# Small matmuls of the recurrent inverse and state chain: one per pair of heads, or one per head in its own column group

## The chip, the cores and the metric

The kernel runs on one core of a Trainium2 chip. The metric is the device time of one launch in microseconds (us), median of three runs; lower is better.

## What is computed

One decoder layer over 528 tokens (16 meta tokens and 512 tokens of the input) of width 2048. A normalised input goes through one large projection. Half of its columns feed sixteen RWKV-7 heads of width 64, the other half eight differential-attention heads; both results are gated, joined, projected again, normalised and added to the input. Cut to what matters here, the recurrent half is, for each head,

```python
def step(S, inp):
    r_t, w_t, k_t, v_t, kk_t, b_t = inp
    sa = jnp.einsum('bhvk,bhk->bhv', S, -kk_t)
    S = S * w_t[:, :, None, :] + sa[..., None] * b_t[:, :, None, :] + v_t[..., None] * k_t[:, :, None, :]
    y = jnp.einsum('bhvk,bhk->bhv', S, r_t)
    return S, y
_, ys = lax.scan(step, S0, (tm(r), tm(decay), tm(k), tm(v), tm(kk), tm(b)))
```

The kernel does this scan by chunks of 64 tokens: in each chunk a triangular 64x64 matrix has to be inverted for each head, and the states go from chunk to chunk.

## The kernel before

The matmul engine (PE) multiplies in two kinds of instruction: a load of the stationary operand into its 128x128 array, and a matmul that streams the moving operand past it. In the profile each plain fp32 matmul of the code stands as two load records and two matmul records; one of type fp32r (a rounded fp32) or fp16 stands as one of each.

**Projections.** `feature_tile` (L547) is most of PE's work: for 65 tiles of 128 output features it takes 16 slices of the contraction, each with three products (high times high, high times low, low times high), all 128 rows by 128 columns, streaming 528 tokens as two matmuls of 264 or 512 tokens as one. The output projection (L807 to L809, L870 to L872) does the same with 512 columns at a time.

**The recurrent part** is done for pairs of heads, eight pairs in all (`NP_`), one pair in each iteration of an outer list `ITER`, while the features of the next pair are projected. The two heads of a pair lie in the top 64 and the bottom 64 partitions (`halves`). Of the 9 chunks (`NC`) each `GC` = 3 make a group, so there are 24 groups in the kernel.

- `inv_pe` inverts the matrices of one group. For each chunk the two heads' 64x64 matrices stand as the diagonal blocks of one 128x128 block matrix, whose other blocks are zero. All its tensors (`x16`, `xt16`, `z16`, `ab_hi`, `ab_lo`, `lv`, fp16) are 3 x 128 = 384 columns wide. After six fp32 matmuls with 64 rows and 128 columns (L646) comes a first transposition (L653), then five levels, each with three matmuls into `zz` (L667), three into `x` (L679) and three into `xt` (L686), a residual with nine (L692 to L694) and a last product with six (L700, L701). Between them VectorE (DVE, `inv_dve`: L1499, L1511, L1514) and ScalarE (ACT, `inv_act`: L1036, L1059, L1062) take the results out of the accumulator `ma`.
- `chain_pe` carries the state. For each chunk it has five fp32 matmuls 128x128x128: g (L723), a first part of the output (L725, not in the first chunk), u (L728), the new state (L733, not in the last chunk) and a second part of the output (L736, not in the first). `chain_dve` and `chain_act` (L1523, L1528, L1538, L1081, L1088) take the results out of `mb`.

**What sets the order.** Every engine's program is a fixed list, written out by generators. Each step of `inv_pe` and `chain_pe` yields a place, and `upto` emits it between two products of a projection, when the projection has come to that place (`feature_tile` calls it after each product, `place - 1 + part / 3`). So PE leaves the projection for one step, does its 1 to 9 small matmuls and goes back. Semaphores (`wait_ge`) hold a step until its operands are there. For one group `inv_pe` has 13 such steps with matmuls that the change touches: the transposition, five times `zz`, five times `x` and `xt` together, the residual, the last product. `chain_pe` has three for each chunk: g with the first output part, u, and the state with the second output part.

Of the kernel before, what the change touches and what calls it, by code (L numbers as in the profile page):

```python
# [34 lines left out]
P = 128  # L35
# [7 lines left out]
HD = 64  # L43
# [40 lines left out]
def constants():  # L84
# [12 lines left out]
    levels = [ident]  # L97
    m = 1
    while m < CH:
        levels.append(same & ((s // (2 * m)) == (t // (2 * m))) & ((s // m) % 2 == 0) & ((t // m) % 2 == 1))  # L100
        m *= 2
    levels[1] = levels[1].astype(np.float32) - ident
    inside = np.broadcast_to((np.arange(TP) % CH != 0)[None, :], (P, TP))
    f16 = np.concatenate(levels + [inside, -ident], 1).astype(np.float16)
# [19 lines left out]
def hybrid_layer(nc, x, meta_tokens, pre_norm_w, w_in, rwkv_mu, rwkv_w0, rwkv_w_up, rwkv_a0, rwkv_a_up,  # L124
# [3 lines left out]
    with ctx:  # L128
# [14 lines left out]
        c16 = sb("c16", [P, (2 + LEVELS) * P + TP], F16)  # L143
# [56 lines left out]
        t_t = several(2, "t_t", GC * P)  # L200
        b_in = several(NG, "b_in", GC * 2 * P)
        b_in3 = [v.rearrange("p (c t) -> p c t", c=GC) for v in b_in]
        b_in5 = [v.rearrange("p (c k h t) -> p c k h t", c=GC, k=2, h=2) for v in b_in]
        state0 = carve("rwkv", "state0", HD)
        g_sb = carve("rwkv", "g_sb", P)
# [6 lines left out]
        lv = carve("rwkv", "lv", (LEVELS - 1) * GC * P, F16)  # L212
        ab_hi = carve("rwkv", "ab_hi", GC * P, F16)
        ab_lo = carve("rwkv", "ab_lo", GC * P, F16)
        x16 = carve("rwkv", "x16", GC * P, F16)
        xt16 = carve("rwkv", "xt16", GC * P, F16)
        z16 = carve("rwkv", "z16", GC * P, F16)
# [47 lines left out]
        def c16v(k):  # L265
            return c16[:, k * P:(k + 1) * P]

        ident, ident16 = c32v("ident"), c16v(0)
        inside = c16[:, (1 + LEVELS) * P:(1 + LEVELS) * P + TP]
        minus16 = c16[:, (1 + LEVELS) * P + TP:]  # L270
        level_masks = c16[:, P:(1 + LEVELS) * P].rearrange("p (l t) -> p l t", l=LEVELS)
# [262 lines left out]
        def _(pe):  # L534
# [100 lines left out]
            def inv_pe(i, g):  # L635
                n = groups_so_far(i, g)
                cs = [g * GC + c for c in range(GC)]
                bl = lambda v, c: v[:, c * P:(c + 1) * P]
                bank = lambda k, c: ma[:, k * 512 + c * P:k * 512 + (c + 1) * P]
# [12 lines left out]
                for c in range(GC):  # L652
                    last = mm(bank(0, c), bl(xt16, c), ident16, start=True, stop=True)  # L653
                last.then_inc(s("t0_done"), 1)
                for c in range(GC):
                    if cs[c] < SC:
                        last = nc.tensor.transpose(bank(1, c), bk[:, cs[c], :], ident)
                last.then_inc(s("bk_turned"), 1)
                for l in range(1, LEVELS):
# [6 lines left out]
                    for c in range(GC):  # L666
# [569 lines left out]
        def _(dve):  # L1236
# [75 lines left out]
            for v in b_in:  # L1312
                V.memset(v, 0.0)
# [384 lines left out]
```

## Time and profile before

| what | us |
|---|---|
| median of 3 runs | 1394.71 (1393.51 to 1394.75) |
| the profiled execution | 1395.48 |
| its span in the profile | 1393.7 |
| PE matmul busy | 1329.2 |
| PE weight load busy | 1136.1 |
| VectorE busy | 731.8 |
| ScalarE busy | 673.1 |
| GpSimd busy | 304.8 |

PE's matmuls are pipelined and their ends are modelled, so two neighbouring records overlap; the distance from one start to the next is what a matmul costs. Times in a timeline are from the start of the span. "x3" in a timeline row means that three records of one form follow one another and are merged into a row.

### The profile page before, as it was taken

The page shows a single profiled execution, that of the slowest core. Times are in us where ns is not written, and L with a number is a line of the kernel's source. Part 1 is how long each engine was busy: PE and PEld are TensorE (multiplying, and loading weights), DVE is VectorE, ACT ScalarE, POOL GpSimd, SP SyncE. Part 2 cuts the span into 40 slices and gives each one's busy share as a digit, 9 for nine tenths or more (in the row PEclk, how much of TensorE's full clock was granted, in tenths as well). Part 3 has the DMA queues.
Part 4 walks back from the last instruction along what each step waited for, and adds up shares of the span by engine and source line. Part 5 has one row for each costly group of instructions (what it writes and reads, how often), then busy time and mean ns, then how long its engine had stood idle before and what let it go on. Part 6 is the DMA issues. An engine that isn't in the chain of part 4 may idle for free.

```text
span 1393.7 us, 24026 instructions
## 1 busy us (share of the span) xinstructions
PE 1329.2 (95%) x9393; PEld 1136.1 (82%) x9393; DVE 731.8 (53%) x1653; ACT 673.1 (48%) x1550; POOL 304.8 (22%) x234
## 2 busy tenths in 40 slices
PE   3999999999999999999999999999999999989997
PEld 3988888797888879889788877898888988768885
DVE  5346767767677686866866433433343333530013
ACT  4435656556565555656555544444443444432331
POOL 3330001000000100001000323333334333334544
PEclk9999999999999999999999998999999999999998
DMA  6221121111112111111112222222222222235333
GB/s 211 71 76 56 47 63 40 56 54 47 56 46 63 47 54 51 51 56 47 53 47 61 83 63 61 71 81 71 75 76 76 69 76 76 67 92 203 109 93 141
DMA packets 151264, 102.24 MB, mean 73 GB/s; under 512 B 6398, under 2 KB 140640, under 8 KB 149600
## 3 DMA queue, kind: packets, MB, share of 16 engines
q1 hardware_dynamic: 151152, 100.71, 24.3%
q8 instruction: 75, 1.23, 0.4%
q14 instruction: 37, 0.30, 0.1%
HBM read 96.49 MB, written 4.19 MB: 72 GB/s over the span
## 4 chain that ended last, share of the span: by engine, by line
PE 83%; DVE 9%; ACT 4%; issue 3%; POOL 1%; DMA 0%; DVEq 0%; ACTq 0%; SPq 0%
PE tile L547 48%; PE tile L807 2%; PE tile L808 2%; PE tile L809 2%; PE ma L773 2%; PE ma L646 2%; PE ma L686 1%; PE ma L679 1%; PE mb L788 1%; PE ma L667 1%; DVE arena L1499 1%; PE mb L790 1%; PE ma L809 1%; PE mb L807 1%; PE ma L807 1%
## 5 line engine op out<-in xcount | busy, mean ns | idle before, releaser
L547 PE MATMUL tile<-hn_hi,w_hi 128*128 128x264 f32 (+1 forms) x1696 | 446.6, 326 | 0.3
L547 PE MATMUL tile<-hn_hi,w_lo 128*128 128x264 f32 (+1 forms) x1696 | 438.6, 322 | 2.2 <-ACT arena L1062 2.2
L547 PE MATMUL tile<-hn_lo,w_hi 128*128 128x264 f32 (+1 forms) x1696 | 437.8, 321 | 0.0
L885 ACT CAST w_hi<-w_raw 128x512 fp32r<-128x512 f32 x324 | 200.4, 619 | 365.3 <-PE tile L547 254.9
L1177 POOL TENSOR_TENSOR w_lo<-w_raw,w_hi 128x512 fp32r<-128x512 f32 x196 | 255.1, 1302 | 448.3 <-ACT w_hi L885 448.2
L547 PEld LDWEIGHTS tile<-hn_hi,w_hi 128*128 128x128 f32 x1696 | 276.5, 190 | 29.2 <-issue 10.2
L547 PEld LDWEIGHTS tile<-hn_hi,w_lo 128*128 128x128 f32 x1696 | 276.3, 190 | 18.8 <-ACT arena L1062 3.6
L547 PEld LDWEIGHTS tile<-hn_lo,w_hi 128*128 128x128 f32 x1696 | 276.2, 190 | 11.6 <-issue 2.2
L1192 POOL TENSOR_TENSOR arena<-arena,power 128x10 f32<-128x10 f32 (+3 forms) x28 | 43.9, 1569 | 620.3 <-DVE arena L1356 471.2
L1499 DVE TENSOR_TENSOR arena<-ma,c 128x384 f16<-128x384 f32 x120 | 66.7, 556 | 45.9 <-PE ma L667 44.6
L1436 DVE TENSOR_TENSOR w_lo<-w_raw,w_hi 128x512 fp32r<-128x512 f32 x128 | 87.5, 683 | 1.3
L1059 ACT ACTIVATE arena<-ma 128x384 f16<-128x384 f32 x120 | 58.8, 490 | 46.3 <-PE ma L679 45.0
L1599 DVE TENSOR_SCALAR arena<-mb,arena 128x128 f32<-128x128 f32 x32 | 11.2, 350 | 91.9 <-PE mb L790 91.9
L807 PE MATMUL tile<-w_hi,hn_hi 128*128 128x512 f32 x128 | 53.1, 415 | 5.5 <-DVE hn_lo L1618 5.5
L1062 ACT ACTIVATE arena<-ma 128x384 f16<-128x384 f32 x120 | 58.3, 486 | 0.0
L808 PE MATMUL tile<-w_lo,hn_hi 128*128 128x512 f32 x128 | 51.6, 403 | 0.0
L809 PE MATMUL tile<-w_hi,hn_lo 128*128 128x512 f32 x128 | 51.5, 403 | 0.0
L1483 DVE TENSOR_TENSOR arena<-arena,c 128x384 f16<-128x384 f16 x144 | 49.0, 350 | 0.8
L1587 DVE TENSOR_TENSOR ma<-ma,c 128x128 f32<-128x128 f32 x32 | 9.6, 299 | 75.1 <-PE mb L773 75.1
L679 PE MATMUL ma<-arena 128*128 128x128 f16 x360 | 41.7, 224 | 3.3 <-DVE arena L1499 2.0
L667 PE MATMUL ma<-arena 128*128 128x128 f16 x360 | 41.6, 224 | 3.2 <-ACT arena L1059 3.1
L1075 ACT ACTIVATE arena<-arena 64x64 f32<-64x64 f32 x112 | 38.5, 344 | 12.0 <-DVE arena L1538 11.2
(262 smaller groups left out, 2090.1 us busy)
## 6 DMA issues: line engine op xcount, KB each, us to landing
w_raw<-w_in SPq DMA_DIRECT2D x260, 256.0 KB, 2.8
w_raw<-w_out SPq DMA_DIRECT2D x64, 256.0 KB, 3.0
big<-x SPq DMA_DIRECT2D x4, 1024.0 KB, 8.0
arena<-x SPq DMA_DIRECT2D x4, 1024.0 KB, 8.6
out<-big SPq DMA_DIRECT2D x3, 1024.0 KB, 3.9
arena<-post_norm_w SPq DMA_DIRECT2D x1, 1024.0 KB, 5.0
out<-big SPq DMA_DIRECT2D x2, 512.0 KB, 3.2
arena<-table_rope SPq DMA_DIRECT2D x2, 264.0 KB, 2.9
```

Of the source, the lines that this page charges most:

```text
L547: last = mm(o[:, at:at + n], w[:, slot, cols], t[:, kt, tok:tok + n], start=(kt == 0 and w is w_hi and t is hn_hi), stop=(kt == KT - 1 and ...
L667: last = mm(bank(0, c), bl(lv, (l - 1) * GC + c), bl(x16, c), start=True, stop=True)
L679: last = mm(bank(0, c), bl(xt16, c), bl(z16, c), start=True, stop=True)
L807: mm(banks[t], hn_hi[:, k, y], w_hi[:, k % RING, :], start=(k == 0), stop=False)
L808: mm(banks[t], hn_hi[:, k, y], w_lo[:, k % RING, :], start=False, stop=False)
L809: last = mm(banks[t], hn_lo[:, k, y], w_hi[:, k % RING, :], start=False, stop=(k == KT - 1))
L885: nc.scalar.copy(w_hi[:, slot, :], w_raw[:, slot, :]).then_inc(s("hi_done"), 1)
L1059: A(x16, ma[:, 0:W], ACT.Copy).then_inc(s("x_taken"), 1)
L1062: A(xt16, ma[:, 512:512 + W], ACT.Copy).then_inc(s("xt_taken"), 1)
L1177: T(w_lo[:, slot, :], w_raw[:, slot, :], w_hi[:, slot, :].bitcast(F32), ALU.subtract).then_inc(s("lo_done"), 1)
L1436: TT(w_lo[:, slot, :], w_raw[:, slot, :], w_hi[:, slot, :].bitcast(F32), ALU.subtract).then_inc(s("lo_done"), 1)
L1499: TT(g3(z16), g3(ma[:, 0:W]), every(ident16), ALU.add).then_inc(s("zz_taken"), 1)
```

## The change

Every small matmul of `inv_pe` behind L646, and every one of `chain_pe`, is split in two, one for each head. The output of one goes to partitions 0 to 63 and that of the other to 64 to 127; its stationary operand has 64 columns. In the inverse, in u and in the second output part the contraction is over the 64 partitions of that head alone, so that the two matmuls take opposite quarters of the array (64 rows by 64 columns). In g, the first output part and the state the contraction stays over 128 partitions (128 rows by 64 columns, one for each half of the columns). All of them stream 64 columns. The inverse's tensors keep only the two diagonal blocks, the heads one above the other, and are 3 x 64 = 192 columns wide; so are `t_t` and the parts of `ma` and `mb` that DVE and ACT read. The constants in fp16 shrink alike, the zeroing of `b_in` at the start goes, and the output's copy in `chain_act` is one instruction and not two. The transposes (L657, L674) and L646 stay as they are, and so do all places.

```diff
+                each = [(c, rows) for c in range(GC) for rows in halves]
+                bl = lambda v, c, rows: v[rows, c * CH:(c + 1) * CH]
+                bank = lambda k, c, rows: bl(ma[:, k * 512:(k + 1) * 512], c, rows)
...
-                for c in range(GC):
-                    last = mm(bank(0, c), bl(xt16, c), ident16, start=True, stop=True)
+                for c, rows in each:
+                    last = mm(bank(0, c, rows), bl(xt16, c, rows), ident16[rows, :], start=True, stop=True)
...
-                    for c in range(GC):
-                        last = mm(bank(0, c), bl(lv, (l - 1) * GC + c), bl(x16, c), start=True, stop=True)
+                    for c, rows in each:
+                        last = mm(bank(0, c, rows), bl(lv, (l - 1) * GC + c, rows), bl(x16, c, rows), start=True,
+                                  stop=True)
...
-                    for c in range(GC):
-                        last = mm(bank(0, c), bl(xt16, c), bl(z16, c), start=True, stop=True)
+                    for c, rows in each:
+                        last = mm(bank(0, c, rows), bl(xt16, c, rows), bl(z16, c, rows), start=True, stop=True)
...
-                    for c in range(GC):
-                        last = mm(bank(1, c), bl(z16, c), bl(xt16, c), start=True, stop=True)
+                    for c, rows in each:
+                        last = mm(bank(1, c, rows), bl(z16, c, rows), bl(xt16, c, rows), start=True, stop=True)
...
-                    mm(bank(0, c), bl(ab_hi, c), bl(x16, c), start=True, stop=False)
-                    mm(bank(0, c), bl(ab_lo, c), bl(x16, c), start=False, stop=False)
-                    last = mm(bank(0, c), minus16, bl(x16, c), start=False, stop=True)
+                    for rows in halves:
+                        mm(bank(0, c, rows), bl(ab_hi, c, rows), bl(x16, c, rows), start=True, stop=False)
+                    for rows in halves:
+                        mm(bank(0, c, rows), bl(ab_lo, c, rows), bl(x16, c, rows), start=False, stop=False)
+                    for rows in halves:
+                        last = mm(bank(0, c, rows), minus16[rows, :], bl(x16, c, rows), start=False, stop=True)
...
-                    mm(bank(1, c), bl(x16, c), ident16, start=True, stop=False)
-                    last = mm(bank(1, c), bl(r16, c), bl(xt16, c), start=False, stop=True)
+                    for rows in halves:
+                        mm(bank(1, c, rows), bl(x16, c, rows), ident16[rows, :], start=True, stop=False)
+                    for rows in halves:
+                        last = mm(bank(1, c, rows), bl(r16, c, rows), bl(xt16, c, rows), start=False, stop=True)
...
-                    mm(o, ar3[:, ch, 0:P], home, start=True, stop=True).then_inc(s("g_done"), 1)
+                    for rows in halves:
+                        last = mm(o[rows], ar3[:, ch, rows], home[:, rows], start=True, stop=True)
+                    last.then_inc(s("g_done"), 1)
                     if ch > 0:
-                        mm(yo, home, ar3[:, ch, P:2 * P], start=True, stop=False)
+                        for h, rows in enumerate(halves):
+                            mm(yo[rows], home[:, rows], ar5[:, ch, 1, h, :], start=True, stop=False)
...
-                    mm(o, t_t[b][:, c * P:(c + 1) * P], g_sb, start=True, stop=True).then_inc(s("u_done"), 1)
+                    for rows in halves:
+                        last = mm(o[rows], t_t[b][rows, c * CH:(c + 1) * CH], g_sb[rows], start=True, stop=True)
+                    last.then_inc(s("u_done"), 1)
...
-                        mm(o, bk_tok[g][:, c * P:(c + 1) * P], home, start=True,
-                           stop=True).then_inc(s("s_done"), 1)
+                        for h, rows in enumerate(halves):
+                            dims = slice(c * P + h * HD, c * P + (h + 1) * HD)
+                            last = mm(o[rows], bk_tok[g][:, dims], home[:, rows], start=True, stop=True)
+                        last.then_inc(s("s_done"), 1)
                     if ch > 0:
-                        last = mm(yo, home, b_in3[g][:, c, P:2 * P], start=False, stop=True)
+                        for rows in halves:
+                            last = mm(yo[rows], home[rows, rows], b_in[g][rows, c, 1, :], start=False, stop=True)
...
-                W = GC * P
+                W = GC * CH
...
-            for v in b_in:
-                V.memset(v, 0.0)
```

## Rows read from the trace of the kernel before

**Rows 1.** The page: busy time, granted clock, the chain that ended last, by engine.

```profile
PE 1329.2 (95%) x9393; PEld 1136.1 (82%) x9393; DVE 731.8 (53%) x1653; ACT 673.1 (48%) x1550; POOL 304.8 (22%) x234
...
PEclk9999999999999999999999998999999999999998
...
PE 83%; DVE 9%; ACT 4%; issue 3%; POOL 1%; DMA 0%; DVEq 0%; ACTq 0%; SPq 0%
```

**Rows 2.** Who PE's matmuls waited for: us in total, times, longest us.

```profile
PE ma L686 <- ACT arena L1055: 3.9, 8, 0.9
PE ma L667 <- ACT arena L1059: 3.1, 9, 0.4
PE mb L728 <- DVE arena L1523: 3.0, 8, 0.4
```

**Rows 3.** Groups of PE records by form: count | busy us, mean ns | idle.

```profile
L667 PE MATMUL ma<-arena 128*128 128x128 f16 x360 | 41.6, 224 | 3.2 <-ACT arena L1059 3.1
L723 PE MATMUL mb<-arena 128*128 128x128 f32 x144 | 29.2, 284 | 1.1 <-DVE arena L1538 0.5
...
L736 PE MATMUL mb<-arena 128*128 128x128 f32 x128 | 24.7, 274 | 0.0
```

**Rows 4.** Timeline of PE: start us, length us, line, form, records; steps in 128x128 form.

```profile
303.85 0.40 PE L547 MATMUL tile<-hn_hi,w_lo 128*128 128x264 f32 x2
304.09 0.35 PE L667 MATMUL ma<-arena 128*128 128x128 f16 x3
304.25 0.49 PE L547 MATMUL tile<-hn_hi,w_hi 128*128 128x264 f32 x2
304.57 0.41 PE L547 MATMUL tile<-hn_lo,w_hi 128*128 128x264 f32 x2
304.82 0.39 PE L728 MATMUL mb<-arena 128*128 128x128 f32 x2
304.96 0.49 PE L547 MATMUL tile<-hn_hi,w_lo 128*128 128x264 f32 x2
305.29 0.41 PE L547 MATMUL tile<-hn_hi,w_hi 128*128 128x264 f32 x2
```

**Rows 5.** Timeline of PE around L646, matmuls with 64 rows.

```profile
324.49 0.41 PE L547 MATMUL tile<-hn_hi,w_lo 128*128 128x264 f32 x2
324.83 0.94 PE L646 MATMUL ma<-arena 64*128 64x128 f32 x12
325.69 0.52 PE L547 MATMUL tile<-hn_hi,w_hi 128*128 128x264 f32 x2
326.05 0.40 PE L547 MATMUL tile<-hn_lo,w_hi 128*128 128x264 f32 x2
```

**Rows 6.** Timeline of PE around the attention scores, L773, matmuls with 64 rows.

```profile
870.38 0.40 PE L547 MATMUL tile<-hn_hi,w_lo 128*128 128x264 f32 x2
870.71 0.60 PE L773 MATMUL ma<-arena 64*128 64x400 f32 x1
870.72 0.60 PE L773 MATMUL mb<-arena 64*128 64x400 f32 x1
871.15 0.50 PE L773 MATMUL ma<-arena 64*128 64x400 f32 x1
...
871.59 0.51 PE L547 MATMUL tile<-hn_hi,w_hi 128*128 128x264 f32 x2
871.93 0.41 PE L547 MATMUL tile<-hn_lo,w_hi 128*128 128x264 f32 x2
```

**Rows 7.** Weight loads by form: busy us, mean ns.

```profile
L728 PEld LDWEIGHTS mb<-arena 128*128 128x128 f32 x144 | 23.7, 189 | 8.0 <-DVE arena L1523 6.2
...
L667 PEld LDWEIGHTS ma<-arena 128*128 128x128 f16 x360 | 20.6, 98 | 22.1 <-issue 12.3 <-ACT arena L1059 6.6
```

**Rows 8.** ScalarE's groups by form: copies out of the accumulators.

```profile
L1059 ACT ACTIVATE arena<-ma 128x384 f16<-128x384 f32 x120 | 58.8, 490 | 46.3 <-PE ma L679 45.0
...
L1088 ACT ACTIVATE arena<-mb 64x192 f32<-64x192 f32 x32 | 10.4, 324 | 3.6 <-PE mb L736 2.9
```

More of the change, by code:

```diff
@@ L96, in constants @@
     f32 = np.concatenate([ident, masks, centre, block, heads, heads / HD, causal], 1).astype(np.float32)
-    levels = [ident]
+    row = s % CH
+    one = (row == col).astype(np.float32)
+    levels = [one]
     m = 1
     while m < CH:
-        levels.append(same & ((s // (2 * m)) == (t // (2 * m))) & ((s // m) % 2 == 0) & ((t // m) % 2 == 1))
+        levels.append((row // (2 * m) == col // (2 * m)) & ((row // m) % 2 == 0) & ((col // m) % 2 == 1))
         m *= 2
-    levels[1] = levels[1].astype(np.float32) - ident
+    levels[1] = levels[1].astype(np.float32) - one
     inside = np.broadcast_to((np.arange(TP) % CH != 0)[None, :], (P, TP))
-    f16 = np.concatenate(levels + [inside, -ident], 1).astype(np.float16)
+    f16 = np.concatenate(levels + [inside, -one], 1).astype(np.float16)
     pos = np.arange(L, dtype=np.float32)
@@ L1085, in chain_act @@
                 lo, w = (g * GC + c0 - 1) * CH, (GC - c0) * CH
-                y4 = mb[:, 512:512 + GC * P].rearrange("p (c h t) -> p c h t", c=GC, h=2)
-                for h, rows in enumerate(halves):
-                    last = A(ysum[rows, lo:lo + w].rearrange("p (c t) -> p c t", t=CH), y4[rows, c0:, h, :], ACT.Copy)
-                last.then_inc(s("y_taken"), 1)
+                A(ysum[:, lo:lo + w], mb[:, 512 + c0 * CH:512 + GC * CH], ACT.Copy).then_inc(s("y_taken"), 1)
             def attn_act(i, gn):
@@ L1475, in inv_dve @@
                 for h, rows in enumerate(halves):
-                    ins = masked(b_in5[g][rows, :, :, h, :], rows, h)
+                    ins = masked(b_in[g][rows], rows, h)
                 ins.then_inc(s("ab_taken"), 1)
                 dve.wait_ge(s("ab_taken"), n)
-                ab32 = b_in3[g][:, :, 0:P]
-                every = lambda m: m.unsqueeze(1).broadcast_to([P, GC, P])
+                ab32 = b_in[g][:, :, 0, :]
+                every = lambda m: m.unsqueeze(1).broadcast_to([P, GC, CH])
                 steps(TT(g3(ab_hi), ab32, every(ident16), ALU.subtract))
@@ L1535, in chain_dve @@
                             dst = suv[rows, chunk_home(i, ch + 1, late), rows]
-                            src, w = mb[rows, rows], w_end_of(i, late)[rows, ch:ch + 1]
+                            src, w = mb[rows, 0:CH], w_end_of(i, late)[rows, ch:ch + 1]
                             if ch:
```

55 lines of the change are left out of this document (25 added, 30 removed).

## The prediction, made before the changed kernel had run

> **What bounds the kernel now.** I read the page first, then who PE waited for, then PE's groups by form, and then PE's own timeline. The page [rows 1] gives PE's matmuls 95% of the span and 83% of the chain that ended last, with the granted clock at its upper level (2.4 GHz, 0.9 or more of it as a mean of a slice) in all but two slices, which read 8; no other engine is over 53%. The waits of PE behind the recurrent steps are short: the three longest add up to 10.0 us [rows 2], all of them to about 15. So nearly every nanosecond that PE's list of instructions needs is a nanosecond of the end, in both directions, and the question is what one step costs PE. The busy times of the groups [rows 3] can't tell that, because records overlap (a mean of 224 ns for a matmul that starts 58 ns behind the one before it). What counts is the distance between starts.
>
> **What a step costs today.** A pair of projection matmuls with 264 columns takes 0.24 us from start to start (303.85 to 304.09) [rows 4]. From the start of the pair before a step to that of the second pair behind it, two pairs (0.48) would have passed anyway; the rest is the step. Three fp16 matmuls (L667): 303.85 to 304.57, 0.72 - 0.48 = 0.24 us. One fp16 matmul takes about 0.058, three take 0.17, so 0.07 is overhead: the long weight load of the next projection has only a short matmul to hide under. One fp32 matmul, two records of 0.11 (L728): 304.57 to 305.29, again 0.24, overhead 0.02; I count it as 0.23 and 0.01, since rows are rounded.
>
> **What a step costs in another form of the array.** The trace of before already has steps whose matmuls use only 64 rows. L646 has twelve records, six on each half of the rows: 324.49 to 326.05 is 1.56, less 0.48 is 1.08 us [rows 5]. The halves do run at once: in L773 the two heads' matmuls start 0.01 apart (870.71, 870.72) and the next two together 0.44 later [rows 6]. So L646 has six turns of 0.11, 0.66 in all, and 0.42 are overhead. L773 has two turns: 870.38 to 871.93 is 1.55, less 0.48 is 1.07; a turn is 0.44 less the 0.11 of a first weight load that nothing hides, so 0.33, two are 0.66, and 0.41 are overhead. Two lengths, one overhead. Its parts show: the way in is 0.34 from the pair before to L646 where 0.24 is usual, the first load is exposed (0.11), the way out has 0.20 from the last record's start (0.86 from the first L646 to the projection, less the exposed load and five turns), and the pair behind takes 0.36 [rows 5]. PE empties itself on the way in and on the way out and can't load weights ahead across the border. No step in 128x128 form shows this [rows 4].
>
> The Trainium skill, TensorEngine Tiling, section Tiling Modes (Key Properties), says that changing the tiling mode drains TensorE, while its section Theoretical Speedup promises up to twofold for a dimension of 64 or less. By the first this change pays at each step; by the second alone it would gain (third rival). The trace agrees with the first at L646 and L773; the page has no price for it, and the sum here uses the rows' price.
>
> **The change, step by step.** All the inverse's matmuls become 64 rows by 64 columns, as u and the second output part do; g, the first output part and the state become 128 rows by 64 columns. PE now changes form on the way into nearly every recurrent step and back, since each stands between two projection products.
>
> Overhead of such a visit: 0.41 as in rows 5 and 6, less 0.05 as the exposed first load has half the columns, plus 0.05 as the way out stays at 0.20 from the last start while the last turn covers only 0.06 of it and not 0.11. I take 0.40.
>
> Turns of the inverse: two heads at once, 64 columns. Before, one matmul was 0.058. The stream is half as long, but the load may not be: the fp16 load in its 128-column form is a short one (98 ns against 189 for fp32) [rows 7], and no row has a 64-column one. From below, half: 0.029; from above, the heads one after the other, 0.116. I take 0.058, unchanged, because half a fp32 load is 0.055 and in rows 6 the halves start together.
>
> - Inverse: 13 steps in each of 24 groups, 312. Each: 0.40 - 0.07 = +0.33. Sum **+103 us**. Its 1512 matmuls cost the same as 1512 pairs.
> - u, 72 steps (L728 has two records each, as L723 has 144 for 72 [rows 3]): 0.40 + 2 x 0.055 - 0.23 = +0.28, **+20**.
> - g with the first output part, 64 steps: 0.40 + 4 x 0.055 - 0.45 = +0.17, **+11**; 8 with g alone at +0.28, **+2**.
> - State and second output part, 56 steps: as before +0.17, and between the two the form changes once more (128 rows to 64), one way out and one exposed load: 0.20, so +0.37, **+21**; 16 with one of them alone at +0.28, **+4**.
>
> That the 128x64 form counts as another form of the array, no row shows; I take the price of the 64-row rows, the nearest ones, and its lower end is none (second rival). For their two heads at once I go by rows 6 too; one after the other would add 0.055 for each of 400 records, 22 us.
>
> **What gets cheaper.** ScalarE's copies out of `ma` go from 384 columns (490 ns) to 192 (324 ns) [rows 8], VectorE's likewise, the second output copy and three memsets at the start go. All of this lies beside PE's work. It reaches the end only through PE's waits: those on the recurrent steps, about 15 us, mostly vanish as the copies shorten and every step gives the other engines 0.3 us more. I take -13; bounds 0 and -30, the latter since waits below the view's threshold would go too. Nothing queued elsewhere is late: weights for the projection (DMA, w_hi, w_lo) are asked for by units used and get more time. What is late next is PE alone.
>
> **Sum.** 103 + 20 + 13 + 25 = 161, less 13 is +148 us on the profiled execution's 1395.5, so 1543.5. The median lies 0.8 below that execution: **1543 us**. The forecast's own bounds: the fp16 turn at 0.045 rather than 0.058 gives 20 less, heads in turn in the 128x64 forms 22 more, waits 15 either way: 1500 to 1585.
>
> **The rivals.**
> 1. *The two heads don't run at once.* All pairs in turn: 1512 x 0.058 = 88 and 336 x 2 x 0.055 = 37 more, **1668**. For it: no row has two 64x64 quarters on a diagonal. Against: rows 6. Chance 0.13.
> 2. *The 128x64 forms are no change of form.* Then 64 steps fall from +0.17 to -0.23, 16 from +0.28 to -0.11 or so, and 56 lose the inner border, 0.20: 26 + 4 (the 8 steps of the second part alone stay) + 11 = 41 less, **1502**. For it: only rows are cut in rows 5 and 6, never columns. Chance 0.20.
> 3. *Faster.* The overhead is that of the fp32 64x128 form, and PE goes into quarters and back without emptying. Then 336 fp32 matmuls save 0.11 each, 37 us, and the waits 13: **1345**; with fp16 turns at half as well, 44 less, 1301. It decides from an overhead of (37 + 13) / 528 visits = 0.095 us; the rows show 0.41 less what is there anyway, at two places. Chance 0.07. The Trainium skill's page TensorEngine Tiling, section Theoretical Speedup, stands behind this one.
> 4. *The clock falls to 1.2 GHz in places, as PE now idles in short gaps.* Gaps of 0.2 us in L646 and L773 leave the granted clock at 0.9 or more in the slices where they lie [rows 1]. Chance 0.02, no price.
>
> **How the numbers follow.** Forecast 0.58, rivals 0.13, 0.20, 0.07, 0.02. The range takes in the second rival, and with it half fp16 turns in part: 1465. Above it takes in the forecast with most of the turns in sequence, 1630, and leaves the first and third outside: 2 in 10. A difference of 0.2% (2.8 us) is about what a measurement can tell from none. Faster 0.07, within 0.2% 0.01, slower 0.92.
>
> **What would show it.** In the profile of the changed kernel: the row of L667's successor should have six records, the pair before it 0.34 to its start, the pair behind it 0.35, and a whole step near 0.57 us where it was 0.24; the two heads' records should start 0.01 apart. PE's matmul busy share should fall, with idle time put down to "issue" and not to another engine. DVE's and ACT's groups of 128x384 should stand as 128x192 at some 350 and 330 ns. The waits of rows 2 should be gone. If a step around L728 costs 0.12 us or less, the third rival holds; if steps with g show no wider borders and those with u do, the second; if three pairs of fp16 take 0.35 us from first to last, the first.

## The result, and the profile after

The changed kernel takes **1455.51 us** (median of 4 runs, 1453.87 to 1456.2) against 1394.11 (4 runs, 1393.46 to 1394.75) for the kernel before on the same chip: ratio 1.044, 95% interval 1.0424 to 1.0455. It is 61 us slower. The direction was forecast; the size was not: +148 was expected, and 1455.5 lies below the range of 1465 to 1630.

The page of after, against [rows 1]: the span, the busy times, and the chain that ended last, by engine.

```profile
span 1454.2 us, 28367 instructions
...
PE 1402.7 (96%) x11577; PEld 1122.4 (77%) x11577; DVE 674.2 (46%) x1650; ACT 629.4 (43%) x1526; POOL 306.6 (21%) x234
...
PE 92%; DVE 3%; ACT 2%; issue 1%; POOL 1%; DMA 0%; DVEq 0%; SPq 0%; ACTq 0%
```

PE has 2184 more matmul records; the recurrent ones stream half as many columns each. It stands as *busier* (96% against 95%) in a longer span: a pair of the projection stands with 0.40 us whether 0.24 or 0.34 us pass to the next start (the timelines of [rows 4] and below), so the time lost between two starts is covered by a record, and no idle time appears. DVE and ACT are each some 50 us less busy, and the end came later all the same: neither bounds this kernel.

Waits of PE's matmuls in after, against [rows 2] (us in total, times, longest us):

```profile
PE ma L686 <- ACT arena L1068: 2.9, 8, 0.9
...
PE ma L665 <- ACT arena L1072: 0.3, 1, 0.3
PE mb L737 <- DVE arena L1531: 0.2, 1, 0.2
```

The waits for ACT's copy and DVE's g copy went from 3.1 and 3.0 to 0.3 and 0.2; that on L686 hardly moved, 3.9 to 2.9.

Groups of after by form (count, then busy us, mean ns, idle us), against [rows 3], [rows 7] and [rows 8]:

```profile
L665 PE MATMUL ma<-arena 64*64 64x64 f16 x720 | 33.6, 199 | 0.3 <-ACT arena L1072 0.3
...
L665 PEld LDWEIGHTS ma<-arena 64*64 64x64 f16 x720 | 20.3, 106 | 27.8 <-issue 16.6 <-ACT arena L1072 0.8
...
L1507 DVE TENSOR_TENSOR arena<-ma,c 128x192 f16<-128x192 f32 x120 | 42.7, 356 | 73.1 <-PE ma L665 72.7
L1072 ACT ACTIVATE arena<-ma 128x192 f16<-128x192 f32 x120 | 39.8, 331 | 59.0 <-PE ma L679 58.0
```

The copies are as short as expected (331 ns for ACT, where it was 490). A load of half the columns stands with 106 ns, no shorter than the 98 of the full one.

What counts is again the distance between starts. PE's timeline in after, against [rows 4] (start us, length us, line, form, records):

```profile
139.79 0.40 PE L544 MATMUL tile<-hn_hi,w_lo 128*128 128x264 f32 x2
140.13 0.28 PE L665 MATMUL ma<-arena 64*64 64x64 f16 x6
140.34 0.51 PE L544 MATMUL tile<-hn_hi,w_hi 128*128 128x264 f32 x2
140.70 0.40 PE L544 MATMUL tile<-hn_lo,w_hi 128*128 128x264 f32 x2
141.03 0.34 PE L729 MATMUL mb<-arena 128*64 128x64 f32 x4
141.20 0.29 PE L733 MATMUL mb<-arena 128*64 128x64 f32 x4
141.41 0.51 PE L544 MATMUL tile<-hn_hi,w_lo 128*128 128x264 f32 x2
141.76 0.41 PE L544 MATMUL tile<-hn_hi,w_hi 128*128 128x264 f32 x2
142.10 0.28 PE L679 MATMUL ma<-arena 64*64 64x64 f16 x6
142.22 0.26 PE L686 MATMUL ma<-arena 64*64 64x64 f16 x6
142.41 0.51 PE L544 MATMUL tile<-hn_lo,w_hi 128*128 128x264 f32 x2
142.75 0.41 PE L544 MATMUL tile<-hn_hi,w_lo 128*128 128x264 f32 x2
```

All borders are there: each pair ahead of a step lasts 0.34 from its start to the step's, where 0.24 is usual. Each pair behind takes 0.34 to 0.36; but that is not all border, because behind a step in 128x128 form it takes 0.33 already (median of before, 0.32 in [rows 4]). With 0.48 taken off for two undisturbed pairs, a `zz` step takes 140.70 - 139.79 - 0.48 = 0.43, g with the first output part 0.58, `x` with `xt` 0.51. Medians over all steps of a kind, with 264 columns in the projection, us:

| step | before | after | difference | forecast |
|---|---|---|---|---|
| `zz` (3 turns) | 0.246 | 0.411 | +0.165 | +0.33 |
| `x`, `xt` (6 turns) | 0.420 | 0.503 | +0.083 | +0.33 |
| residual (9 turns) | 0.583 | 0.599 | +0.016 | +0.33 |
| u | 0.228 | 0.461 | +0.233 | +0.28 |
| g, first output part | 0.447 | 0.580 | +0.133 | +0.17 |
| state, second output part | 0.448 | 0.725 | +0.277 | +0.37 |

Each step at the median of its kind, summed over both traces, gives +31 us for the inverse and +42 for the chain. The time inside the steps beyond those medians, which is waits, went from 38 to 17 (-21). Everything between the steps is 9 longer. 31 + 42 - 21 + 9 = 61, the difference of the spans (60.5). The terms depend somewhat on what is counted as one kind: another grouping gives +30, +44 and -20, and so 6 between the steps. (One kind hides a wait in its median; this is taken up in the account of the inverse's steps below.)

**The clock.** Part of the time between the steps is the clock. Windows of after (us, busy us and records of each engine, granted clock, share of the DMA engines, GB/s):

```profile
140.00:146.80 6.80, 6.80 (x80) 5.59 (x78) 3.51 (x12) 2.74 (x9) 0.67 (x1) 1.00 0.15 41
146.80:153.60 6.80, 6.80 (x42) 4.31 (x42) 1.44 (x4) 3.86 (x11) 1.30 (x1) 0.50 0.13 39
153.60:160.40 6.80, 6.80 (x93) 5.72 (x93) 4.46 (x11) 3.90 (x9) 0.00 (x0) 1.00 0.15 41
```

In the middle one the granted clock is 0.50, the lower level of 1.2 GHz, and PE gets through 42 records where it has 80 and 93 beside it. The timeline around its start:

```profile
144.57 1.28 PE L613 MATMUL tile<-c,arena 128*128 128x2 f32 x10
145.71 0.49 PE L544 MATMUL tile<-hn_hi,w_lo 128*128 128x264 f32 x2
...
146.92 0.81 PE L544 MATMUL tile<-hn_lo,w_hi 128*128 128x264 f32 x2
147.53 0.64 PE L544 MATMUL tile<-hn_hi,w_lo 128*128 128x264 f32 x2
```

From 146.8 the pair behind a step takes 0.61, where 0.35 is usual, and the next one, ahead of a step, 0.57 (147.53 to 148.10) and not 0.34. Ahead of it PE did five fp32 matmuls of 2 columns, ten records (L613, 1.14 us), among the recurrent steps. There are five such stretches in after, from 146.8, 239.0, 334.5, 515.5 and 699.8 us, 31 us in all; between 120 and 790 us the mean granted clock (third column from the end) is 1.00 in before and 0.98 in after:

```profile
120.00:790.00 670.00, 652.95 (x5439) 563.41 (x5437) 472.23 (x1097) 383.70 (x906) 33.97 (x21) 1.00 0.19 54
```

That is before's; the same window of after:

```profile
120.00:790.00 670.00, 667.87 (x7020) 509.02 (x7019) 389.47 (x1023) 311.97 (x814) 26.58 (x14) 0.98 0.17 48
```

PE stands as busy in all but 2 us of it: its busy share doesn't show this loss. What a fall costs can be read from after alone. From one run of the ten small records to the next, one pair of heads later, PE takes 90.5 us where the clock does not fall, 92.0 with a fall of 3.4 us and 93.3 to 93.4 with one of 6.8. So a short fall costs 1.5 us and a long one 2.9, and the five together, four of them long, some **13 us**. Not all of that is a difference from before: behind 790 us, and ahead of the last fall at the very end, before is at the lower level for 20 us in four falls and after for 14 in two.

### The profile page after: what moved, and what is told of

Its sections match the earlier page's. It is cut to its first block, busy times and chain, and to the rows that moved or that the text cites. A ratio compares the mean times of both kernels' runs of the same rounds, so it can differ in the third digit from the quotient of the medians.

```text
span 1454.2 us, 28367 instructions
## 1 busy us (share of the span) xinstructions
PE 1402.7 (96%) x11577; PEld 1122.4 (77%) x11577; DVE 674.2 (46%) x1650; ACT 629.4 (43%) x1526; POOL 306.6 (21%) x234
## 4 chain that ended last, share of the span: by engine, by line
PE 92%; DVE 3%; ACT 2%; issue 1%; POOL 1%; DMA 0%; DVEq 0%; SPq 0%; ACTq 0%
PE tile L544 57%; PE tile L820 2%; PE tile L822 2%; PE tile L821 2%; PE ma L665 2%; PE ma L679 2%; PE ma L786 2%; PE ma L644 1%; PE mb L737 1%; PE mb L801 1%; PE mb L729 1%; PE mb L745 1%; PE mb L749 1%; PE mb L803 1%; PE ma L686 1%
## 5 line engine op out<-in xcount | busy, mean ns | idle before, releaser
L544 PE MATMUL tile<-hn_lo,w_hi 128*128 128x264 f32 (+1 forms) x1696 | 443.7, 325 | 0.0
L1507 DVE TENSOR_TENSOR arena<-ma,c 128x192 f16<-128x192 f32 x120 | 42.7, 356 | 73.1 <-PE ma L665 72.7
L1072 ACT ACTIVATE arena<-ma 128x192 f16<-128x192 f32 x120 | 39.8, 331 | 59.0 <-PE ma L679 58.0
L1531 DVE COPY arena<-mb 128x64 f32<-128x64 f32 x72 | 16.0, 222 | 64.0 <-PE mb L729 63.2
L1546 DVE SCALAR_TENSOR_TENSOR arena<-mb,arena 64x64 f32<-64x64 f32 x112 | 31.7, 283 | 26.2 <-PE mb L745 24.8
L1479 DVE TENSOR_TENSOR arena<-ma,c 64x384 f32<-64x384 f32 x48 | 26.6, 555 | 36.7 <-PE ma L644 36.4
L665 PEld LDWEIGHTS ma<-arena 64*64 64x64 f16 x720 | 20.3, 106 | 27.8 <-issue 16.6
```

The source lines that it names most:

```text
L544: last = mm(o[:, at:at + n], w[:, slot, cols], t[:, kt, tok:tok + n], start=(kt == 0 and w is w_hi and t is hn_hi), stop=(kt == KT - 1 and ...
L665: last = mm(bank(0, c, rows), bl(lv, (l - 1) * GC + c, rows), bl(x16, c, rows), start=True, stop=True)
L1072: A(x16, ma[:, 0:W], ACT.Copy).then_inc(s("x_taken"), 1)
L1507: TT(g3(z16), g3(ma[:, 0:W]), every(ident16), ALU.add).then_inc(s("zz_taken"), 1)
```

## Experiments

The theory behind them: PE empties itself at each change of form, and this, paid twice for each visit, is more than the smaller matmuls give back. In the first group the parts of the change are taken singly and the border is priced by itself; then borders are saved in the changed kernel; then the halved stream is had without a border. All kernels compute the full result; e3 and e4 do extra matmuls whose output is overwritten.

**The inverse alone, the chain alone.** e1 has after's inverse and before's chain (its `t_t` and `b_in` are written in block form by two half copies each); e2 has before's inverse and after's chain. The core of e1's edit to after (u alone; g, the output parts and the state likewise):

```diff
-                    for rows in halves:
-                        last = mm(o[rows], t_t[b][rows, c * CH:(c + 1) * CH], g_sb[rows], start=True, stop=True)
-                    last.then_inc(s("u_done"), 1)
+                    mm(o, t_t[b][:, c * P:(c + 1) * P], g_sb, start=True, stop=True).then_inc(s("u_done"), 1)
```

> The inverse alone in 64x64 quarters with compact tensors; the chain as before (128x128), for which VectorE writes t_t and b_in in block form by halves. The forecast of before priced this part at +103 us. Theory A (a border costs the drain: +0.09 us on the way in, the last matmul's own stream plus 0.09 on the way out, and an fp16 turn of two heads takes 0.034 instead of 0.058) gives, from the steps as the changed kernel's trace shows them (zz 0.41 for 0.25, x and xt 0.50 for 0.42, residual 0.60 for 0.58), +30 us less what waits give back: +20 to +30. Rival B (the extra time is the doubled count of instructions, not the borders) gives for 1512 more matmuls a share of 1512/2184 of the whole, +42.

> The chain alone with one matmul for each head; the inverse as before (128x128, block tensors). The forecast of before priced this part at +58 us. Theory A: u +0.23, g with output +0.13, state with output +0.28 us for each of 72, 64 and 56 steps, and the single ones: +43 us, less few waits: +36 to +44; with the inverse alone it adds up to the whole change, +61, within 5 us. Rival B (count of instructions) gives 672/2184 of the whole, +19.

Measured: e1 1405.53 against 1393.34 (1.009, 1.0075 to 1.0105), +12. e2 1428.35 against 1393.34 (1.0258, 1.0234 to 1.0283), +35. So the chain, with 216 of the 528 visits, carries three quarters of what the two cost. That speaks against the rival of both expectations, in which the number of matmuls makes the time: it asked for +42 for the inverse and +19 for the chain, the other way round. Both results lie below their ranges. The inverse's own step medians say +31, and its shorter copies take back most of the waits, which the expectation for e1 counted too low.

The two add up to 47, and the whole is 61, so they don't add up as expected. Two things need both parts. The first is that a wait can be given back only once. The time that steps take beyond the median of their kind is 32 us in before, 12 in e1, 22 in e2 and 12 in after (grouped otherwise than in the sum above, hence 32 and 12 for its 38 and 17): alone the parts give back 20 and 10, together 20. For one pair of heads with no fall of the clock, the times are 84.3 us in before, 85.7 in e1, 87.8 in e2 and 90.5 in after; the whole exceeds the sum of its parts by 1.3, some 10 us for the eight pairs. The second is the clock: between 120 and 790 us it never falls in e1, it falls for 7 us in e2 and for 31 in after. Two of e2's four runs took 1425 us and two 1431, so the 14 is itself good to a few us.

**The border by itself.** Ahead of each of before's 528 recurrent steps e3 puts three matmuls of one quarter of the array, e4 three in 128x128 form that also stream 64 columns:

```diff
+                for _ in range(3):
+                    mm(ma[0:HD, 0:HD], ident16[0:HD, 0:HD], ident16[0:HD, 0:HD], start=True, stop=True)
```

is e3, ahead of the transposition, and at the same place e4 has

```diff
+                for _ in range(3):
+                    mm(ma[:, 0:HD], ident16, ident16[:, 0:HD], start=True, stop=True)
```

> The kernel before, and ahead of each of the 528 steps three more fp16 matmuls of one 64x64 quarter into the region that the step then overwrites. Extra work, the result is the same. Theory A: way in +0.09, three short matmuls 0.05 + 2 x 0.03, way out to the 128x128 form 0.12, first load of it exposed 0.03 to 0.11: 0.35 to 0.45 each, +185 to +235 us. Rival B (only the number of matmuls counts): the same as in the run with three 128x128 ones.

> The kernel before, and ahead of each of the 528 steps three more fp16 matmuls in the 128x128 form that stream 64 columns. Control for the run with the quarter form. Theory A: no border, 3 x 0.03 to 0.058 us each, +48 to +92 us, so the quarter form costs at least 110 us more than this. Rival B: no difference between the two.

Measured: e3 1539.47 against 1393.34 (1.1053, 1.1036 to 1.1069), +146. e4 1439.19 (1.033, 1.0314 to 1.0345), +46. As many matmuls with as many columns, in another form, cost 100 us more, 100 / 528 = **0.19 us** for a border in and a border out. In the medians of the steps it is 0.21 (a `zz` step takes 0.21 more in e3 than in e4, u 0.21, g with the first output part 0.22): e3 has fewer waits left, which hides some 8 us of it. All three results are under what I had given in the expectations (+185 to +235, +48 to +92, at least 110 between them). Timeline of e3, one `zz` step:

```profile
304.13 0.41 PE L547 MATMUL tile<-hn_hi,w_hi 128*128 128x264 f32 x2
304.46 0.28 PE L669 MATMUL ma<-c 64*64 64x64 f16 x3
304.67 0.35 PE L671 MATMUL ma<-arena 128*128 128x128 f16 x3
304.83 0.49 PE L547 MATMUL tile<-hn_lo,w_hi 128*128 128x264 f32 x2
305.16 0.41 PE L547 MATMUL tile<-hn_hi,w_lo 128*128 128x264 f32 x2
```

and of e4, one state step:

```profile
318.37 0.40 PE L547 MATMUL tile<-hn_hi,w_hi 128*128 128x264 f32 x2
318.62 0.26 PE L747 MATMUL mb<-c 128*128 128x64 f16 x3
318.71 0.47 PE L749 MATMUL mb<-arena 128*128 128x128 f32 x2
318.94 0.49 PE L547 MATMUL tile<-hn_lo,w_hi 128*128 128x264 f32 x2
```

In e3 the pair ahead takes 0.33 and the three quarter matmuls 0.21 up to the next start; in e4 0.25 and 0.09. The 0.09 for three is also a price: a matmul that streams 64 columns in 128x128 form, its full load with it, takes 0.03 (46 / 1584 = 0.029 over the whole kernel).

**Fewer borders.** `CHAIN_FROM` places the chain's steps; with 4.21 they fall where the inverse's are, and one visit does both. e5 is this in after, e6 in before:

```diff
-        CHAIN_FROM, CHAIN_STEP = 4.7, 1.0
+        CHAIN_FROM, CHAIN_STEP = 4.21, 1.0
```

> The changed kernel with the chain's places moved by half a step, so that a chain step stands directly behind a step of the inverse and PE goes away from the projection once for both; 207 of the 216 chain steps can pair. Same work, same instructions. Theory A (borders): behind a step in quarters, u needs no border of its own and saves 0.09 + 0.15 + 0.11 us, 69 times, 24 us; g and the state still change to 128x64 inside the pair and save about 0.17 to 0.19, 138 times, 25 us. Together about 50 us faster than the changed kernel, 1405 to 1420, if no wait is new. Rival B (count of instructions): no change, 1455, or slower by new waits.

> The same move of places in the kernel before, where all these steps are 128x128. Control. Theory A: there is no border to save, only the one exposed load behind a step, 207 x 0.01 to 0.03: 2 to 6 us faster, 1388 to 1393, if no wait is new. If the gain here is as large as in the changed kernel, the places and not the borders made it.

Measured: e5 1442.39 (1432.82 to 1449.53) against 1393.41 (1.0346, 1.0291 to 1.0402), 13 less than after. e6 1439.93 (1.0337, 1.032 to 1.0354), 46 more than before. Both expectations missed: I took the merge to cost nothing in before. The answers that PE needs from DVE and ACT for both steps come late, as the waits of e6 show (the first stands at 3.9 us and the second at 2.0 in before):

```profile
PE ma L686 <- ACT arena L1055: 14.4, 15, 1.6
PE ma L679 <- DVE arena L1499: 11.6, 22, 0.8
```

The merge is worth 13 + 46 = 59 us more in the changed kernel, where it saves borders, than in before, where there are none to save. But that is 59 / 207 = 0.28 for each merged visit and includes other things: waits, and the clock, which between 120 and 790 us is at the lower level for 48 us in e5 and for 31 in after. The steps' own medians are cleaner. `zz` with u in one visit takes 0.55 in e5, where the two take 0.41 + 0.46 in after: 0.32 saved. In before the same merge saves 0.01 (0.46 for 0.246 + 0.228). `x`, `xt`, g and the first output part in one visit, where one border stays inside, save 0.20 in e5 (0.89 for 0.503 + 0.580) and nothing in e6 (0.87 for 0.420 + 0.447). The expectation had 0.35 and 0.17 to 0.19.

e7 turns the second output part into a 128x64 matmul, its other operand padded with zeros, so that a step with the state has one form and not two:

```diff
-                        for rows in halves:
-                            last = mm(yo[rows], home[rows, rows], b_in[g][rows, c, 1, :], start=False, stop=True)
+                        for h, rows in enumerate(halves):
+                            last = mm(yo[rows], home[:, rows], b_out[g][:, c, h, :], start=False, stop=True)
```

> The changed kernel, with the second output part over 128 rows and 64 columns (its operand padded with zeros for the other head), as the state in front of it. VectorE has two more copies for each group. Theory A: the border between state and second output part goes, 0.378 becomes 0.23 from first to last start, 56 times: 8 us faster than the changed kernel, 1446 to 1449. If 128x64 and 64x64 were no different forms: no change.

Measured: 1450.33 (1.041, 1.0395 to 1.0426), 5 less than after. It does more arithmetic and is faster: 128x64 and 64x64 are two forms to PE, as 128x64 and 128x128 are. From the first start of a state step to the last it is 0.230 us where after has 0.378, which over 56 steps is the 8 us of the expectation; some 4 of them are lost again, as the transposition now waits for DVE, which has the two added copies ahead of what the transposition needs (16 of 23 such steps have 0.60 us from the pair ahead, where after has 0.34).

**The order of the heads.** The theory held that two quarters overlap because they alternate. e9 does all three matmuls of the top head, then those of the bottom:

```diff
-                each = [(c, rows) for c in range(GC) for rows in halves]
+                each = [(c, rows) for rows in halves for c in range(GC)]
```

> The changed kernel with the inverse's matmuls of a step in another order: first the three of the top head, then the three of the bottom head, where before the heads alternate. Residual and last product stay. Theory A: two heads run at once only if they stand side by side in PE's list, since PE keeps its order: a zz step goes from 3 turns of 0.034 to 5 or 6 of them, +0.06 to +0.10 us in each of 264 steps with 3 pairs (x and xt count for two): 360 groups x 0.06 to 0.1 = +22 to +36 us on 1455. If PE overlaps them from anywhere in its queue: no change.

Measured: 1456.97 against 1393.56 (1.0453, 1.0437 to 1.0468), which is after's time. The `x` and `xt` of one step in e9:

```profile
142.83 0.29 PE L679 MATMUL ma<-arena 64*64 64x64 f16 x6
142.95 0.26 PE L686 MATMUL ma<-arena 64*64 64x64 f16 x6
```

Six records start in 0.12 us, the same as in after (142.10 to 142.22). They start in pairs, 0.010 us apart in e9 and 0.003 in after, while the three matmuls that e3 puts into one and the same quarter start 0.053 and 0.031 us apart: pairs are a sign of two quarters. That part of my picture was wrong: the overlap doesn't need an alternating list.

**What brings the clock down.** In after PE ran the five matmuls of 2 columns (ten records) in one go before the clock fell. e12 emits them one by one between projection products:

```diff
                 for m in range(TG):
+                    yield NORM_AT + 0.34 * (m + 1)
                     last = mm(o[:, 2 * m:2 * m + 2], rkp[:, m * P:(m + 1) * P], c32v("heads"), start=True, stop=True)
```

> The changed kernel, and the ten matmul records with 2 columns (the norm's sums, L613) no longer stand in one bunch but two by two between products of the projection. In the changed kernel the granted clock falls to 0.5 five times between 147 and 707 us of the span, each time at or right behind this bunch, 31 us in all; in the kernel before, never there. Theory A: quarters, borders and this bunch together let PE's work thin out; with the bunch spread the falls go, and as projection pairs take 0.60 instead of 0.24 us in them, some 13 to 15 us with them, less 5 new exposed loads and starts in 8 stretches, 3 us: 10 us faster than the changed kernel, 1442 to 1448. Rival B: the falls come from quarters and borders alone and stay: 1455 to 1460.

Measured: 1448.21 against 1393.58 (1.0385, 1.0368 to 1.0403), 7 less than after. The window from 120 to 790 us in e12:

```profile
120.00:790.00 670.00, 666.41 (x7118) 509.23 (x7116) 392.74 (x1034) 314.06 (x824) 26.56 (x14) 0.99 0.17 48
```

Two falls of 3.4 us are left of 31 us. So the run of tiny matmuls brings the clock down only together with the recurrent steps in their new forms around it (before has the same ten records and no fall there). The saving fits the price above: 13 us for the five falls, less 3 for the two that are left, less 2 because a pair of heads without a fall takes 90.8 us in e12 and 90.5 in after, is 8, and 7 were measured. What exactly PE's work has to look like for a fall these runs don't settle: e3 has about as many borders as after, and in the same window one fall of 3.4 us.

**Half the stream without a border.** The blocks can stay 128x128 on the stationary side while the moving side is compact: 64 columns with the heads one above the other. The product is then compact too, and what is used as a stationary operand next has to be expanded.

```diff
-                        last = mm(bank(0, c), bl(lv, (l - 1) * GC + c), bl(x16, c), start=True, stop=True)
+                        last = mm(slim(0, c), bl(lv, (l - 1) * GC + c), cl(xc16, c), start=True, stop=True)
```

e8 does this in all of the inverse, expanding on DVE and ACT. e10 does it for all but `xt` and the last product, expands `z` by one DVE multiplication with a mask, and asks for `xt_taken` only ahead of `x`. e11 has that later wait alone:

```diff
-                    if l > 1:
-                        pe.wait_ge(s("xt_taken"), n * 5 + (l - 1 - 5))
...
                     yield level_at(g, l, 1)
+                    if l > 1:
+                        pe.wait_ge(s("xt_taken"), n * 5 + (l - 1 - 5))
```

> The kernel before with the inverse in the 128x128 form throughout, so without any border, but with compact moving operands: the stationary operand is the block matrix of both heads, the moving one and the result are 64 columns wide. ScalarE and VectorE write xt and z twice, compact and as blocks by halves. The chain is as before. Theory A: the gain of the quarters was never the quarters but the halved stream; the control run showed 0.029 us for a 128x128 matmul with 64 columns, so 1512 x (0.058 - 0.029) = 44 us less on PE. Copies cost ScalarE some 0.33 and VectorE some 0.15 us more for each level; if that stays beside PE, 1350 to 1365; if PE waits for the blocks, up to 1395. Rival B: instructions are as many as before, so no change.

> As the run with compact moving operands in 128x128 form, but only where that costs few copies: x and zz are compact, xt stays as before; z is made compact by VectorE and then spread to blocks by one product with a mask; the wait for the copy of xt stands ahead of the matmuls that need it and no longer behind zz. Theory A: 42 of 63 matmuls for each of 24 groups stream half, 1008 x 0.029 = 29 us less on PE; ScalarE has 0.16 us less for each level, VectorE 0.15 more. If the waits of PE stay as before: 1362 to 1370; if the longer way from zz to xt is late, up to 1390. Rival B: no change.

> The kernel before with only the move of that wait (from behind zz to ahead of x). Control for the run before. PE waits some 2 to 8 us in total for this copy ahead of projection matmuls; 1386 to 1393.

Measured: e8 1399.19 against 1393.41 (1.0043, 1.0028 to 1.0058). Its `zz` step is 0.193 and `x` with `xt` 0.308, less than before's 0.246 and 0.420, but the time that steps lose to waits rises from 38 to 66 us. The waits of e8:

```profile
PE tile L552 <- ACT arena L1084: 13.7, 24, 0.9
PE ma L696 <- DVE arena L1526: 6.7, 22, 0.4
```

They say where: the copies by ACT that end in L1084, for which PE waits 24 times, once for each group, and DVE's second copy. The expectation's 1350 to 1365 held only if none of this was waited for. e10 takes both off the path: **1375.46 us** (1374.3 to 1376.83) against 1393.56, ratio 0.9866 (0.9849 to 0.9882). It beats both kernels, by 1.3% against before. It lies above the 1362 to 1370 that I had worked out for unchanged waits and below the 1390 for late ones. e11 takes 1391.6 (0.9984, 0.9975 to 0.9993), so the later wait accounts for 2 of e10's 18 us. The busy times on the page of e10:

```profile
PE 1306.5 (95%) x9393; PEld 1114.9 (81%) x9393; DVE 753.3 (55%) x1797; ACT 671.3 (49%) x1598; POOL 305.1 (22%) x234
```

One of its steps with `x` and `xt` in PE's timeline:

```profile
304.13 0.41 PE L552 MATMUL tile<-hn_hi,w_hi 128*128 128x264 f32 x2
304.38 0.27 PE L687 MATMUL ma<-arena 128*128 128x64 f16 x3
304.49 0.34 PE L695 MATMUL ma<-arena 128*128 128x128 f16 x3
304.63 0.49 PE L552 MATMUL tile<-hn_lo,w_hi 128*128 128x264 f32 x2
304.96 0.40 PE L552 MATMUL tile<-hn_hi,w_lo 128*128 128x264 f32 x2
```

It has as many matmuls as before (9393), the pair ahead of this step takes 0.25, so there is no border, and the step costs 0.83 - 0.48 = 0.35 where it was 0.42. DVE has 22 us more of work, beside PE's, and the time that steps lose to waits is 44 us, 6 more than in before.

## Why the prediction was right in kind and wrong in size

**What bounds the kernel: right.** PE's own list is the end. DVE and ACT lost some 50 us of work each, and the end moved with PE's steps alone.

**PE empties at a border: right, and right about the way in.** The pair ahead takes 0.34 in every step of the timeline of after, as in [rows 5]. Rows of before with 64 rows of the array priced forms that before doesn't have (quarters, half the columns), and e3 against e4 confirms the border by itself, 0.19 us for the two. That PE empties is the reading of these distances; no row shows the array itself.

**"The way out stays at 0.20 from the last start": the first step that failed.** Measured from the last start to the next projection, it is 0.120 in fp16 and 0.148 to 0.152 in fp32. It isn't a constant. In L646, from which I took it [rows 5], 0.11 of the 0.20 was the last matmul's own turn. [Rows 6] spoke against it already: 871.15 to 871.59 is 0.44, and the matmul's own turn there is 0.33. The rule that fits all four is own turn plus about 0.09 to 0.11. I had instead *added* 0.05 because a short turn covers less. Against a visit of 0.40 the way out beyond its turn is 0.05 less, the first load (0.026 exposed, where 0.06 was counted) and the pair behind another 0.04. In the inverse's 312 visits these are 16 and 12 us; in the chain's 216, where only the way out is off, 11, and 3 more on the border inside a step (from the first start to the last, a state step went from 0.332 to 0.378, and 0.05 of the forecast 0.20 was too much).

**"I take 0.058, unchanged" for a turn: the second, and the largest term.** Three turns take 0.090 from the first start to the last and six take 0.185, so a turn of both heads is 0.095 / 3 = 0.032 us. The lower bound in the text, 0.029, was nearly it. 1512 x 0.026 = 39 us. The reason given for 0.058, that half a fp32 load is 0.055, took the price of one type for another; [rows 7] had shown fp16 loads at half the fp32 ones, and the step to half the columns of *those* was not made. The nearest row for a bound was the wrong one. That the load record stands with 106 ns says nothing of its price: most of it lies under another record.

**Inverse and chain together.** 39 + 16 + 12 = 67 of the 72 by which +103 exceeded +31, and 11 + 3 = 14 of the 16 by which +58 (20 + 13 + 25) exceeded +42. Some 3 of the missing 5 are a wait in disguise. Where `zz` is followed by two transposes, 16 steps, the medians seem to say that the step got cheaper (0.613 to 0.581). But in before eight of these steps wait and take 0.80 or more, the other eight take 0.41, and 0.613 lies between the two groups; in after all but one take 0.58. Without waits such a step is 0.17 dearer, like any other `zz` step. Counted so, the inverse has +34 and the waits -24, and the total stays.

**Waits: right, too small.** -13 was forecast, -21 measured (-24 by the count just given). The bound of -30 held. But the longest of the three, on L686, stayed, so not "mostly vanish" by the rows named; the rest came from waits below the view's threshold.

**The rivals.** The first (heads in turn, 1668) is refuted: the two records of a pair start 0.003 to 0.008 us apart in nearly all pairs of every form. The second (128x64 no change of form, 1502) is refuted: L729's pair ahead takes 0.33 like the others, and a g step grew by 0.133; its time was nearer than the forecast's, by another error. The prediction had no row in which the columns are cut. The trace of before has one, and it would have spoken for this rival:

```profile
797.85 0.27 PE L780 MATMUL ma<-c,arena 128*128 128x128 f32 x1
797.96 0.27 PE L782 MATMUL ma<-c,arena 128*16 128x128 f32 x1
797.99 0.49 PE L547 MATMUL tile<-hn_hi,w_hi 128*128 128x264 f32 x2
```

L782, a transposition, uses 128 rows and 16 columns, and the projection starts 0.03 us behind it: no border. So fewer columns in use are not enough for one. What sets L782 apart from L729, which has 64 and pays, no run here tests.

The third (faster) holds, with the prediction's turns, only below 0.095 us of overhead for each visit; with the measured turns and waits it would hold below (37 + 39 + 21) / 528 = 0.18, so the packing came nearer to paying than the text made it look. A border in and out takes 0.19 (e3 against e4), a visit with two forms pays a third border, and the steps grew by 73 us though their turns shrank. The Trainium skill, TensorEngine Tiling, section Tiling Modes (Key Properties), says that a change of mode drains the engine, and each border here agrees. The same page's section Theoretical Speedup gives up to twofold for a dimension of 64 or less; the turn went from 0.058 to 0.032, which agrees, though e4 has 0.029 for as few streamed columns in 128x128 form, and the borders take more than the gain.

The fourth (the clock) had a chance of 0.02 and no price, and came about beside the forecast: 13 us of falls between 120 and 790 us. The row that it was dismissed by could not have shown it. A slice of [rows 1] is 35 us long, so a fall of 3.4 us leaves it at 0.95 and one of 6.8 at 0.90, which both read 9. The kernel before has falls of its own, the first two here, and of all slices only the one with most of the second reads 8 apart from the last; the page of after reads 9 in all forty:

```profile
792.20:795.60 3.40, 3.40 (x18) 3.40 (x17) 0.50 (x3) 3.33 (x9) 0.54 (x1) 0.50 0.27 77
833.20:843.40 10.20, 6.26 (x24) 5.12 (x24) 4.23 (x6) 1.26 (x4) 2.23 (x2) 0.50 0.10 27
```

**The sum, redone.** 148 - 72 - 16 - 8 + 9 = 61: the inverse, the chain, the waits, and the time between the steps. That the 9 are the clock is likely and not shown: part of the 13 us of falls lies inside steps, and behind 790 us before has more of them than after. The range missed because its lower end was the second rival with "half fp16 turns in part", 78 below the forecast; turns, way out and waits, all on one side, are 96. The errors of a constant that is multiplied by 528 don't average out. Two sums of the text are off by little: its own bounds come to 1508 and 1580, not 1500 and 1585, and in the second rival 16 steps at 0.39 are 6 us and not 4.

**What would show it**: the six records, the borders, the copies (356 and 331 ns) came as said. "A step near 0.57" was 0.43. "PE's busy share should fall, with idle time put down to issue" was wrong: time lost at a border stands as busy, in this profile, in the records beside it.

## What to carry to other kernels

Before small matmuls are packed into parts of the array, count how often PE has to go there and back: each round trip costs about 0.2 us, and one that does three short matmuls doesn't earn it, while one of nine about breaks even here (+0.016 us). Where such matmuls stand between full-array ones, keep the block-diagonal operand stationary and halve only the moving one; the stream shrinks by the same half with no border (-1.3% here, where packing cost 4.4%), as long as the expansion of the result stays off the path of PE (e8, where it didn't, is 0.4% slower than before). And split an overhead taken from a row into its parts, of which the last matmul's own turn is one, before multiplying it by several hundred.

## What the runs showed of the chip

- A fp16 matmul of 64 columns in 128x128 form, with its own full load, takes 0.029 us in a run of such (e4); two 64x64 ones, one for each head, take 0.032 (after).
- Two quarters of the array on its diagonal overlap even when the list names one head's matmuls first (e9: pairs 0.010 us apart). Two 128x64 halves that alternate in the list overlap too (after: 0.007 us apart).
- 128x128, 128x64 and 64x64 are three forms, and going between any two of them costs a border (L665 and L729 in after; e7). A 128x16 matmul among 128x128 ones costs none (L782 in before, 0.03 us to the next start).
- The granted clock fell to 0.5 for 31 us in a stretch where PE's records leave hardly a gap, and not in the kernel before, whose busy share there is lower (652.95 against 667.87 of 670 us). A fall of 6.8 us cost 2.9 us, one of 3.4 cost 1.5.
